# One stage of a two-block network on one core: v centred and turned for two chunks at once, a second buffer for u and v, squared outputs kept elsewhere

## The reference

```python
def step(state, inp):
    r_t, w_t, k_t, v_t, a_t, b_t = inp
    sa = jnp.einsum("bhvk,bhk->bhv", state, a_t)
    state = (state * w_t[:, :, None, :] + sa[..., None] * b_t[:, :, None, :]
             + v_t[..., None] * k_t[:, :, None, :])
    return state, jnp.einsum("bhvk,bhk->bhv", state, r_t)
...
mean = jnp.mean(y, axis=-1, keepdims=True)
var = jnp.mean(jnp.square(y - mean), axis=-1, keepdims=True)
y = (y - mean) * lax.rsqrt(var + GN_EPS)
```

## Time and profile before

| | before |
|---|---|
| median of three runs | 1992.55 us (1986.46 to 1995.49) |
| profiled execution: span | 1985.2 us |
| profiled execution: own time | not given beside its span |
| PE busy | 1943.4 us, 98% of the span |
| DVE, ACT, POOL busy | 72%, 46%, 6% |
| scan, 468 to 562 us: PE, DVE, ACT busy | 90.10, 65.19, 32.50 us of 94 |
| read from HBM | 410.60 MB |

### The profile page before, as it was taken

One profiled execution on the slowest core, in us unless ns is written; L12 is line 12 of the kernel. 1 busy time (PEld: TensorE's weight loads), 2 busy tenths in 40 slices (PEclk: granted clock), 3 DMA queues, 4 the chain that ended last, 5 costly groups with the idle time before them and its releaser, 6 DMA issues.

```text
span 1985.2 us, 32865 instructions
## 1 busy us (share of the span) xinstructions
PE 1943.4 (98%) x12898; PEld 1682.0 (85%) x12898; DVE 1435.0 (72%) x2025; ACT 907.8 (46%) x1476; POOL 123.0 (6%) x126
## 2 busy tenths in 40 slices
PE   7999999999999999999999999999999999999998
PEld 5888888888988878888888888888888888888887
DVE  7997959334769988888877775444477967767876
ACT  3346221142335455555555554444464546545553
POOL 0000002000024200000000000000010000002200
PEclk8999999999999999999999999999999999999999
DMA  9996424564529756666555556555535545446553
GB/s 394 421 420 212 153 84 161 218 235 170 190 96 423 290 194 229 251 233 241 205 190 188 184 182 230 185 187 181 206 143 182 190 149 191 149 149 233 185 183 120
DMA packets 58936, 418.34 MB, mean 211 GB/s; under 512 B 6673, under 2 KB 7057, under 8 KB 12561
## 3 DMA queue, kind: packets, MB, share of 16 engines
q1 hardware_dynamic: 52210, 366.59, 50.1%
q0 software_dynamic: 6336, 46.14, 6.0%
q10 hardware_dynamic: 288, 4.19, 0.5%
HBM read 410.60 MB, written 6.29 MB: 210 GB/s over the span
## 4 chain that ended last, share of the span: by engine, by line
PE 88%; DVE 6%; DMA 3%; issue 2%; ACT 1%; POOL 1%; SPq 0%; DVEq 0%; ACTq 0%; POOLq 0%
PE ps L716 43%; PE ps L717 22%; PE ps L693 10%; PE ps L833 2%; DMA bk<-in_ada 2%; DVE ar L1913 1%; DMA zb<-in_ada 1%; PE ps L828 1%; PE ps L975 1%; PE ps L1105 1%; PE ps L964 1%; PE ps L874 1%; POOL h L600 0%; DVE bk L1720 0%; PE ps L1180 0%
## 5 line engine op out<-in xcount | busy, mean ns | idle before, releaser
L716 PE MATMUL ps<-x_pair,whi 128*128 128x512 f32 x2464 | 876.8, 400 | 5.3 <-issue 2.8
L717 PE MATMUL ps<-x_pair,wlo 128*128 128x256 f32 x2464 | 692.2, 281 | 0.0
L1742 DVE TENSOR_TENSOR wlo<-ring,whi 128x1024 fp32r<-128x1024 f32 x468 | 549.8, 1211 | 104.0 <-ACT whi L1262 99.9
L716 PEld LDWEIGHTS ps<-x_pair,whi 128*128 128x128 f32 x2464 | 463.5, 188 | 124.0 <-issue 12.0
L1262 ACT ACTIVATE whi<-ring 128x1024 fp32r<-128x1024 f32 x468 | 462.7, 1032 | 99.8 <-PE ps L717 97.1
L717 PEld LDWEIGHTS ps<-x_pair,wlo 128*128 128x128 f32 x2464 | 466.1, 189 | 0.3
L1269 ACT ACTIVATE px<-ps 128x256 f32<-128x256 f32 x202 | 77.8, 385 | 460.3 <-PE ps L717 460.3
L716 PE MATMUL ps<-hid_pair,whi 128*128 128x512 f32 x688 | 243.3, 399 | 0.0
L717 PE MATMUL ps<-hid_pair,wlo 128*128 128x256 f32 x688 | 193.2, 281 | 0.0
L716 PEld LDWEIGHTS ps<-hid_pair,whi 128*128 128x128 f32 x688 | 129.3, 188 | 32.4 <-DVE wlo L1742 0.3
L693 PE MATMUL ps<-mixb,ring 128*128 128x256 f32 x640 | 142.4, 385 | 0.0
(11 more groups left out here) (306 smaller groups left out, 2334.4 us busy)
## 6 DMA issues: line engine op xcount, KB each, us to landing
ring<-in_fi SPq DMA_DIRECT2D x86, 1024.0 KB, 4.8
ring<-in_zin SPq DMA_DIRECT2D x52, 1024.0 KB, 4.9
ring<-in_fo SPq DMA_DIRECT2D x32, 1024.0 KB, 4.8
ring<-in_ada SPq DMA_DIRECT2D x26, 1024.0 KB, 6.4
bk<-in_ada SPq DMA_DIRECT2D x22, 1024.0 KB, 18.0
ring<-in_wr SPq DMA_DIRECT2D x16, 1024.0 KB, 4.9
ring<-in_wv SPq DMA_DIRECT2D x16, 1024.0 KB, 4.8
ring<-in_wo SPq DMA_DIRECT2D x16, 1024.0 KB, 9.0
```

The lines of the kernel that those rows point to most:

```text
L716: mm(ps[:, bank, 0:2 * S], w_h, pair_k, start=first and k == 0, stop=False)
L717: m = mm(ps[:, bank, 0:S], w_l, pair_k[:, 0, :], start=False, stop=last and k == n - 1)
L1742: V.tensor_tensor(wlo[:, hf % WB, 0:m], ring[:, u % RING, 1024 * x:1024 * x + m], whi[:, hf % WB, 0:m].bitcast(F32), ALU.subtract).then_in ...
```

## The change

- L975 runs only in chunks 0 and 2, with 128 tokens (two chunks) as stationary tile: the tokens of the even chunk land on partitions 0 to 63, those of the odd one on 64 to 127. As many results are copied, in four pieces: three at once, both chunks' first half (banks 0 and 1) and the even chunk's second half, and the odd chunk's second half only behind the copy to `rr`.
- The odd chunks have their own buffer for u and v, the second half of `zb`.
- For that, the squares of chunk 0 go to `px`, those of chunk 1 to the place of the late constants in `cst`. The load of those constants moves behind the last load of `wo`, with a wait for the head sums.
- SCAN_DOTS goes from (2, 4, 4, 2) to (3, 3, 4, 2).
- Waits: L1003 of an even chunk waits for the third copy of its pair (before, the second copy of the chunk), the new state of an even chunk for the fourth.

```diff
-SCAN_DOTS = (2, 4, 4, 2)
+SCAN_DOTS = (3, 3, 4, 2)
...
-        uv = flat_c[:, 2048:4096]
+        uv2 = (flat_c[:, 2048:4096], zb[:, 2048:4096])
...
-        y_sq = [a.rearrange("p (i t) -> p i t", t=CH) for a in (zb[:, 2048:3072], zb[:, 3072:4096], flat_c[:, 1024:2048],
-                                                                flat_b[:, 0:1024])]
+        px_flat = px[:].rearrange("p n t -> p (n t)")
+        y_sq = [a.rearrange("p (i t) -> p i t", t=CH) for a in (px_flat[:, 0:1024], cst[:, EARLY:EARLY + 1024],
+                                                                flat_c[:, 1024:2048], flat_b[:, 0:1024])]
...
-            sp.dma_start(cst[:, EARLY:], t["const"][:, EARLY:]).then_inc(ld_late, 16)
...
             stream("wo", t["wo"], NT)
+            sp.wait_ge(hs_sum, 9)
+            sp.dma_start(cst[:, EARLY:], t["const"][:, EARLY:]).then_inc(ld_late, 16)
             stream("fi", t["fi"], 2 * FT)
...
             for c in range(NCH):
+                uv = uv2[c % 2]
-                for i in range(NT):
+                for i in range(0 if c % 2 else NT):
                     if i % 8 == 0:
                         pe.wait_ge(e_g, 8 * c + (6 if i else 2))
-                    m = mm(ps[0:CH, i // 4, (i % 4) * P:(i % 4 + 1) * P], mixa[:, i, c * CH:(c + 1) * CH], const("cen"),
+                    m = mm(ps[:, i // 4, (i % 4) * P:(i % 4 + 1) * P], mixa[:, i, c * CH:(c + 2) * CH], const("cen"),
                            start=True, stop=True)
...
+                pe.wait_ge(e_v, 2 * c + 2)
                 if c:
-                    pe.wait_ge(e_v, 2 * c + 1)
                     pe.wait_ge(e_s, c)
...
-                pe.wait_ge(e_v, 2 * c + 2)
+                if c % 2 == 0:
+                    pe.wait_ge(e_v, 2 * c + 3)
...
                 if c < NCH - 1:
+                    if c % 2 == 0:
+                        pe.wait_ge(e_v, 2 * c + 4)
...
             for c in range(NCH):
-                for x in range(2):
-                    act.wait_ge(c_v, 2 * c + x + 1)
-                    A(uv[CH:P, 1024 * x:1024 * (x + 1)], ps[0:CH, 2 * x:2 * x + 2, :].rearrange("p b n -> p (b n)"),
-                      ACT.Copy).then_inc(e_v, 1)
+                def v_half(x, e):
+                    A(uv2[e][CH:P, 1024 * x:1024 * (x + 1)],
+                      ps[CH * e:CH * e + CH, 2 * x:2 * x + 2, :].rearrange("p b n -> p (b n)"), ACT.Copy).then_inc(e_v, 1)
+
+                if c % 2 == 0:
+                    act.wait_ge(c_v, c + 1)
+                    v_half(0, 0)
+                    v_half(0, 1)
+                    act.wait_ge(c_v, c + 2)
+                    v_half(1, 0)
...
                 act.wait_ge(c_r, 2 * c + 1)
                 A(rr.rearrange("p i v -> p (i v)"), ps[:, 0:2, :].rearrange("p b n -> p (b n)"), ACT.Copy).then_inc(e_r, 1)
+                if c % 2 == 0:
+                    v_half(1, 1)
```

More of the change, by code:

```diff
@@ L399, in build @@
         gab5 = gab.rearrange("p (e c i) t -> p e c i t", e=2, c=NCH)
-        uv_e = uv.rearrange("p (i e v) -> p i e v", e=2, v=HD)
+        uv_e2 = [a.rearrange("p (i e v) -> p i e v", e=2, v=HD) for a in uv2]
         gs4 = gs.rearrange("p (i e) t -> p i e t", e=2)
@@ L1461, in _ @@
                 A(rr.rearrange("p i v -> p (i v)"), ps[:, 0:2, :].rearrange("p b n -> p (b n)"), ACT.Copy).then_inc(e_r, 1)
+                if c % 2 == 0:
+                    v_half(1, 1)
                 act.wait_ge(c_u, c + 1)
-                A(uv_e[0:CH, :, 1, :], ps[CH:P, 4:6, :].rearrange("p b n -> p (b n)").rearrange("p (i v) -> p i v", v=HD),
+                A(uv_e2[c % 2][0:CH, :, 1, :], ps[CH:P, 4:6, :].rearrange("p b n -> p (b n)").rearrange("p (i v) -> p i v", v=HD),
                   ACT.Copy).then_inc(e_u, 1)
@@ L1978, in _ @@
                 dve.wait_ge(c_u, c + 1)
-                V.tensor_copy(uv_e[0:CH, :, 0, :], ps[0:CH, 4:6, :].rearrange("p b n -> p (b n)")
+                V.tensor_copy(uv_e2[c % 2][0:CH, :, 0, :], ps[0:CH, 4:6, :].rearrange("p b n -> p (b n)")
                               .rearrange("p (i v) -> p i v", v=HD)).then_inc(e_u, 1)
```

## The result

The changed kernel takes 1985.77 us (median of 13 runs, 1975.39 to 1992.43) against 1992.44 us of the kernel before beside it (13 runs): a ratio of 0.9967, 95% interval 0.9953 to 0.9981. Forecast were 1987.8 us and 4.8 us gained; measured are 6.6 us, with an interval of 3.8 to 9.4 from the ratio. Measured twice more beside other runs of the kernel before, the same kernel gave 0.9984 [0.9969, 0.9999] and 0.9953 [0.9935, 0.9971]. Over all runs of both kernels in the four sets of this study, the 31 runs of the changed kernel have a mean of 1984.1 us and the 103 of the kernel before one of 1989.5: 5.4 us less, +- 1.6.

The account below looks back on a forecast made before the run. PE was taken as the bound, on 88% of the span. Chunk 1 2.66 + chunk 3 2.11 - matmul pace 0.4 + moved constants 0.4 = 4.8 us, so 1992.55 becomes 1987.8 us; range 1981.5 to 1994.

Parts of the forecast that it names:

- What bounds the kernel: Whole kernel and scan: PE holds 88% of the span; time taken from it is gained wherever it is not waiting.
- chunk 1: Scan, transposes after the Grams: without L975 PE waits about 1 us for the DVE's masks; gain 2.66 us, not 3.64.
- Chunk 3: Scan, transposes after the Grams: DVE masks end later against PE, leaving a hole of 1.5 us; gain 2.11 us.
- The pace: Wide centring in chunks 0 and 2: 119 ns a record instead of 114, as the transposes; 0.4 us lost.
- The first rival: Wide centring: the 128-column load is not covered, pace near 165 ns; gain only 1.9 us, 1990.7 us; chance 0.10.
- The covers of parts 2 and 3: ACT's copies and DVE's dots in the scan stay hidden: 0.5 us at L1003, 1.8 in chunk 0, 2.3 in chunk 1.
- Part 5: First stage's last dot: moving the late constants' load lets its own load land sooner; 0.4 us gained, between 0 and 1.25.
- the dip of the DMA share at 149 us: Load queue at 149 to 150 us: share 0.77, taken as mostly caught up, so little gain from the moved constants.
- Rival 2: Head sums and L1028: the clock fall goes too, 1.2 us, plus 0.85 from the constants; 6.9 us, 1985.7; chance 0.12.
- Rival 3: Scan: PE runs out of instructions; one stall with its clock costs 5.6 us, 1993.4; decides from 4.8 us; chance 0.08.
- a sign against it: PE: a new wait put down to issue, over 1 us, would show the forecast wrong.
- The sum: Whole kernel: 2.66 + 2.11 - 0.4 + 0.4 = 4.8 us faster, 1987.8 us; the forecast keeps 0.70.

Follow-up runs that it names:

- dots_2442: The changed kernel with the dots of the scan back at (2, 4, 4, 2) instead of (3, 3, 4, 2); ratio to the kernel before 0.9971.
- narrow_after: The changed kernel with 14 units of weights (12 of the scan's dots, two of g2) loaded 128 of 2048 columns wide; ratio 0.9962, 1978.87 us.
- narrow kernels: The kernel before and the changed kernel, both with 14 units of weights loaded 128 of 2048 columns wide; ratios 0.9990 and 0.9962.
- narrow_state: The changed kernel with state matmuls between the transposes' halves in chunks 1 and 3, and 14 weight units loaded 128 columns wide; ratio 0.9958.
- by_chunk: The changed kernel with the centring alone undone: v centred 64 columns wide in every chunk, with ACT's old copies; ratio 1.0002.
- const_late: The kernel before with one edit: the load of the late constants moved behind the last w_o load; ratio 0.9998.
- state_first: The changed kernel with the state matmuls between the two halves of the transposes in chunks 1 and 3; ratio 0.9984, repeated 0.9975.
- narrow_before: The kernel before with 14 units of weights (12 of the scan's dots, two of g2) loaded 128 of 2048 columns wide; ratio 0.9990, 1985.62 us.
- reordered kernel: The changed kernel with state matmuls between the transposes' halves in chunks 1 and 3: full loads 0.9984 and 0.9975, narrow loads 0.9958.

## Why the prediction was right

**What bounds the kernel, and chunk 1.** Right to the row. PE was the bound at both places, the gain is not the 3.64 us of the removed group but what is left after the DVE's masks: 2.66 forecast, 2.64 measured, with a hole of 0.86 us by its bracket and 1.00 by the starts for the forecast 1.0; the bracket is 0.85 in dots_2442 and narrow_after.

**Chunk 3.** Forecast 2.11. The clean row has 2.21, with a hole of 1.29 us by its bracket, 1.43 by the starts, where 1.5 was expected. In the changed kernel's own trace it is 2.65 with a hole of 0.85, since PE came late to it through an issue wait. The step assumed that nothing ahead of it would move; the wait of 1.20 us at L1034 did.

**The pace.** Mis-sized, on the safe side: 115 ns and not 119, 0.08 us for both pairs and not 0.4. I had taken the transposes as the nearest row for their full tile; the nearer one was the centring itself, for the moving side is the same and the load is covered in both. The first rival is dead: 192 ns a load and the same pace. On the rule of the Trainium skill behind it ("TensorE: Matmul & The Clock Gate", section "Back-to-back issue gap"), that load and matmul together set the spacing, read as the sum of the two, the trace differs at this place: the load grew by 56 ns and the spacing by 1.

**The covers of parts 2 and 3.** Right: 1.86 us for 1.8, 2.27 for 2.3, no wait for ACT at L1007, none for the late u copy. dots_2442 shows that the dot could as well have stayed where it was. Its cover in chunk 1 was forecast to be gone with four dots; chunk 1 lost nothing (12.25 against 12.26 us), so a cover of about zero was enough there.

**Part 5.** The 0.4 us is not borne out: the last dot starts no sooner in the traces with the move (a mean of 173.5 us in eleven, against 173.15 and 173.21 in the two without), and the timing of the move alone gives 0.4 +- 3.6 us. Nothing shows more than the lower bound, 0, to which the dip of the DMA share at 149 us had pointed.

**The rivals.** Rival 2 (the clock fall at the head sums goes) went the other way: it came earlier and lasted longer, and L1034 took 3.70 us instead of 3.29. Its time, 1985.7 us, is nearly the measured 1985.77, but neither of its two terms is there, so that is chance. Rival 3, a stall for want of instructions inside the scan, did come, in the form that the prediction named as a sign against it: 1.61 and 1.20 us, 1.76 more than before. It did not decide, being smaller than the 4.8 us from which it would have. That PE wants for instructions in such a wait is the prediction's name for it; no row shows it. By the narrow kernels it belongs to the scan's loads. The windows do not make it that simple:

```profile
523.00:525.30 2.30, 0.69 (x24) 0.55 (x20) 0.00 (x0) 0.33 (x1) 0.00 (x0) 1.00 0.90 324
...
530.30:531.50 1.20, 0.03 (x1) 0.00 (x0) 1.17 (x2) 0.00 (x0) 0.00 (x0) 1.00 0.00 0
```

The first wait of the changed kernel falls in a DMA share of 0.90, the second in one of 0.00. And narrow_state has one of 1.21 us at its head sums, while a w_o unit, still 1024 KB wide, runs:

```profile
544.00:545.70 1.70, 0.49 (x9) 0.40 (x6) 1.70 (x5) 1.02 (x1) 0.00 (x0) 1.00 0.89 361
```

In both narrow scans none is left behind the first Gram, so the wide loads have a part in them; how, when one of the waits falls where nothing moves, is open.

**The sum.** 4.8 forecast. The clean scan gives 4.8, though by a smaller pace (+0.3), a better chunk 3 (+0.1) and no part 5 (-0.4): that these errors cancel in the total is luck, that chunks 1 and 3 are met within 0.1 is not. The range is not the sum of its terms, which give 1983.5 to 1995.4; the result lies in both. Measured over the whole kernel are 6.6, 3.2 and 9.4 us in three sets, 5.4 +- 1.6 over all runs. The traces of the changed kernel say less against the one of before, 0.7 to 2.5 us at the bonus matmuls. With the other traces at full loads, scan and tail together have a mean of 91.9 us for the old centring (before, by_chunk, const_late) and of 88.8 for the new one (three of the changed kernel and dots_2442): 3.1 us, and the narrow pair has 3.2. So the traces give some 3 us over scan and tail, the timed runs 3.8 at least. Whether the rest is scatter of few traces is not settled: of the timed executions only the span and the mean clock are known. If the tail does lose 1 us by the change, that is a term that the sum does not have.

## What to carry to other kernels

A group of matmuls taken out of a chain on PE is worth its time only up to the next engine's work that ran beside it: find the semaphore that the following group would wait on, and take the later of the two ends. Before counting a hole's filling as gain, look at what follows: state_first bought 2 to 2.6 us in the scan and in the traces paid them back at once behind it, in an issue wait and a longer stretch at half clock, so compare two landmarks on both sides of the clock's fall, not the ends of the group that moved. A single trace holds waits of 0.2 to 2.2 us that come and go between executions; subtract them, with the 0.2 us and more that each costs beyond its bracket, before comparing traces, and take the size of a gain under 0.5% from several sets of timings.

## What the runs showed of the hardware that was not expected

- Records of fp32 matmuls (two to a matmul) with 128 moving columns and a 128-column stationary tile start every 115 ns, with a 64-column one every 114, though the loads take 192 and 136 ns. With 64-column ones that go in turn to the two partition halves they start every 57 ns: 64 in 3.65 us.
- Issue waits on PE stand at fixed records of a program (L1018 after the 18 records of one row in three traces of the changed kernel and in dots_2442, 1.58 to 1.61 us), but at some of these places their length varies: 0.27 and 2.18 us at one record of the same code.
- The clock fell to half among the head sums, matmuls with two moving columns, in each of the 13 traces, with PE busy 2.00 of 2.00 us in the windows shown: 28 head sums, nearly all at half clock, take 2.85 us (102 ns each), 61 at full clock 3.51 us (58 ns each). It lasted some 10 us in all three traces of the reordered kernel and in one of the changed kernel's three, 3.4 us in the kernel before and in narrow_before, and nearly 7 in the other seven traces. What sets the length was not tried.
